# Attention beside chunk products: one place for TensorE's small work in a step, and lone 16-key tiles joined

## What is computed

```python
q, k, v, fg = hn @ w_q, hn @ w_k, hn @ w_v, hn @ w_f + b_forget
for q0, q1 in blocks:              # 16 meta rows, then four blocks of 128 queries
    s = q[q0:q1] @ k[:q1].T * 64 ** -0.5 + cum[q0:q1] - cum[:q1]   # forget gates' log sums
    p = softmax(where(causal, s, -inf))
    out[q0:q1] = p @ v[:q1]        # block [q0, q1) reads keys [0, q1)
```

## Time and profile before

| | us |
|---|---|
| median of 3 runs (911.46 to 912.39) | 911.9 |
| the profiled execution | 911.48 |
| its span, first to last instruction | 909.5 |
| TensorE busy | 900.1 |
| VectorE busy | 614.1 |
| ScalarE busy | 445.0 |
| GpSimd busy | 22.3 |

### The profile page before, as it was taken

One profiled execution on the slowest core, in us unless ns is written; L12 is line 12 of the kernel. 1 busy time (PEld: TensorE's weight loads), 2 busy tenths in 40 slices (PEclk: granted clock), 3 DMA queues, 4 the chain that ended last, 5 costly groups with the idle time before them and its releaser, 6 DMA issues.

```text
span 909.5 us, 13686 instructions
## 1 busy us (share of the span) xinstructions
PE 900.1 (99%) x5039; PEld 784.2 (86%) x5039; DVE 614.1 (68%) x959; ACT 445.0 (49%) x722; POOL 22.3 (2%) x40
## 2 busy tenths in 40 slices
PE   8999999999999999999999999999999999999997
PEld 7999999899999999888888888888888888888886
DVE  7799989999999999987765444533443354334543
ACT  6532246777778777766843244421243133214523
POOL 2010000000000000010000000000000000000000
PEclk9999999999999999999999999999999999999999
DMA  9333332212221222213323532323233333333602
GB/s 267 93 98 92 92 93 70 70 49 70 70 68 48 70 70 54 81 52 92 116 82 104 186 92 85 101 94 100 87 100 108 92 92 92 115 93 98 179 1 93
DMA packets 129466, 84.34 MB, mean 93 GB/s; under 512 B 3103, under 2 KB 118815, under 8 KB 129424
## 3 DMA queue, kind: packets, MB, share of 16 engines
q1 hardware_dynamic: 128192, 82.32, 31.1%
q10 hardware_dynamic: 640, 1.18, 0.4%
q0 software_dynamic: 592, 0.29, 0.2%
HBM read 81.62 MB, written 2.16 MB: 92 GB/s over the span
## 4 chain that ended last, share of the span: by engine, by line
PE 92%; DVE 4%; ACT 2%; issue 1%; DMA 1%; SPq 0%; ACTq 0%
PE pj L1455 41%; PE pQ L1707 19%; PE pj L1451 17%; PE pQ L1585 3%; PE pQ L1602 3%; PE pj L1773 2%; PE pQ L1773 2%; PE pj L1493 1%; DVE cv L1051 1%; PE pQ L1572 1%; PE pQ L1571 1%; DVE w_lo L955 1%; DMA ga<-in_x_dram 1%; ACT w_hi L577 1%; PE pQ L1605 1%
## 5 line engine op out<-in xcount | busy, mean ns | idle before, releaser
L955 DVE TENSOR_TENSOR w_lo<-raw,w_hi 128x1024 fp32r<-128x1024 f32 x129 | 157.6, 1222 | 113.5 <-ACT w_hi L577 113.2
L577 ACT ACTIVATE w_hi<-raw 128x1024 fp32r<-128x1024 f32 x129 | 135.9, 1053 | 161.5 <-PE pQ L1707 121.3
L1455 PE MATMUL pj<-in_hi,w_lo 128*128 128x512 f32 x512 | 201.5, 394 | 0.0
L1455 PE MATMUL pj<-in_lo,w_hi 128*128 128x512 f32 x512 | 200.6, 392 | 0.0
L1455 PE MATMUL pj<-in_hi,w_hi 128*128 128x512 f32 x512 | 200.1, 391 | 0.2 <-DVE w_lo L955 0.2
L1051 DVE SCALAR_TENSOR_TENSOR cv<-u,prm,cv 128x512 f32<-128x512 f32 x240 | 170.6, 745 | 0.5
L1455 PEld LDWEIGHTS pj<-in_hi,w_hi 128*128 128x128 f32 x512 | 96.3, 188 | 19.5 <-DVE w_lo L955 0.6
L1455 PEld LDWEIGHTS pj<-in_lo,w_hi 128*128 128x128 f32 x512 | 96.2, 188 | 17.8
L1455 PEld LDWEIGHTS pj<-in_hi,w_lo 128*128 128x128 f32 x512 | 96.3, 188 | 17.2
L1707 PE MATMUL pQ<-w_hi,mid_hi 128*128 128x512 f32 x256 | 99.8, 390 | 0.0
L1707 PE MATMUL pQ<-w_lo,mid_hi 128*128 128x512 f32 x256 | 99.6, 389 | 0.0
(11 more groups left out here) (206 smaller groups left out, 1226.1 us busy)
## 6 DMA issues: line engine op xcount, KB each, us to landing
raw<-in_w_in_dram SPq DMA_DIRECT2D x57, 512.0 KB, 3.8
raw<-in_w_mlp_up_dram SPq DMA_DIRECT2D x32, 512.0 KB, 4.0
raw<-in_w_mlp_down_dram SPq DMA_DIRECT2D x32, 512.0 KB, 3.8
raw<-in_w_attn_out_dram SPq DMA_DIRECT2D x8, 512.0 KB, 3.6
raw<-in_w_conv_out_dram SPq DMA_DIRECT2D x8, 512.0 KB, 3.6
raw<-in_w_out_dram SPq DMA_DIRECT2D x8, 512.0 KB, 3.9
ga<-in_x_dram SPq DMA_DIRECT2D x4, 512.0 KB, 8.4
cv<-in_x_dram SPq DMA_DIRECT2D x1, 2048.0 KB, 9.1
```

Source lines behind the costliest of these rows:

```text
L577: A(w_hi[:, c % SPLIT, :], raw[:, c % RAW, :], ACT.Copy).then_inc(s_hi, 1)
L955: V.tensor_tensor(w_lo[:, c % SPLIT, :], raw[:, c % RAW, :], w_hi[:, c % SPLIT, :].bitcast(F32), ALU.subtract).then_inc(s_lo, 1)
L1455: last = mm(prod(c), wt, src[:, at:at + NT], **flags)
```

## The change

TensorE: CUTS becomes (0, 4, 12), and everything small stands after unit 4 of a step, in the order transposes, half_out, value transposes, scores. The transposes are now those of the unit two steps back instead of one, and half_out moves from steps 3, 5, 7 and 1 to 4, 6, 0 and 2. The lone tiles: the fifth key tile's 16 probabilities are put by ScalarE into `lone_probs`, behind 32 columns of zeros, and turned from there (48 columns instead of 128); the fifth value tile holds the keys of two lone tiles, 16 rows each at rows 0 and 32. So in the second half_out of a head one product of 256 columns for each part serves block 1's lone tile and block 3's together, and line 1605's products go.

ScalarE and VectorE: other orders in the steps, other numbers of taps, `normalise` of 528 keys and the copy of V in two instructions each. Not shown: four one-column tensors become columns of one, and the same reordering in ScalarE's step of k = 8.

```diff
-TAPS_FIRST_PAIR = (2, 3, 2, 2, 2, 2, 3, 2)
-TAPS_STEP = {18: (3, 4, 1, 2, 1, 2, 3, 2), 19: (3, 4, 1, 2, 2, 2, 3, 2)}
+TAPS_FIRST_PAIR = (3, 4, 2, 2, 1, 3, 1, 2)
+TAPS_STEP = {18: (1, 3, 3, 3, 1, 3, 2, 2), 19: (1, 3, 3, 4, 1, 3, 2, 2)}
...
-FIRST_CELL = (0, 2, 0, 4)
-CELLS = 9
+FIRST_CELL = (0, 2, 0, 5)
+CELLS = 10
+LONE_ROW = 32
...
+        with ExitStack() as row_gap:
+            lone_probs = row_gap.enter_context(nc.sbuf_tensor("lone_probs", [P, LONE_ROW + META], F32))
...
+        def probs_cell(q, t):
+            return lone_probs[:, :] if (q, t) == (QT - 1, QT) else probs(q, t * P, (t + 1) * P)
...
+        def lone_values(c):
+
+            at = AT + 2 * P
+            return pj[:, c % 2, at:at + 4 * P].rearrange("p (a b) -> p a b", b=2 * P)[:, :, 0:META]
...
@@ -671,7 +681,11 @@
                 U = 8 * k + s
                 wait(act, s_rinv, U + 1, it, 16)
                 nk = META + P * (s % QT + 1)
-                A(probs(s % QT, 0, nk), probs(s % QT, 0, nk), ACT.Copy, scale=rinv[:, s:s + 1]).then_inc(s_pn, 1)
+                last = A(probs(s % QT, 0, min(nk, NT)), probs(s % QT, 0, min(nk, NT)), ACT.Copy, scale=rinv[:, s:s + 1])
+                if nk > NT:
+                    last = A(lone_probs[:, LONE_ROW:], probs(s % QT, NT, nk), ACT.Copy,
+                             scale=rinv[:, s:s + 1])
+                last.then_inc(s_pn, 1)
...
-                    A(vT[:, 0:T], prod(c - 1, T), ACT.Copy).then_inc(s_vev, 1)
+                    A(vT[:, 0:NT], prod(c - 1, T)[:, 0:NT], ACT.Copy)
+                    A(vT[:, NT:VT].rearrange("p (a b) -> p a b", b=LONE_ROW)[:, 0:2, 0:META],
+                      lone_values(c - 1), ACT.Copy).then_inc(s_vev, 1)
...
-                if s == 3 and k >= 2:
-                    out_high(k - 2, it)
-                turned_out(s, k, it)
-                if s == 2 and k >= 2:
-                    out_copy(1, k - 2, it)
                 if s == 6:
                     projection_out(s, k, it)
                 if s % 2 == 0 and c > N_PAIR:
                     high(c + 1, it, 8)
+                if s == 2:
+                    if k >= 2:
+                        out_copy(1, k - 2, it)
+                    if live:
+                        values_high(k - 1, it)
+                if s != 6:
+                    turned_out(s, k, it)
+                if s == 3:
+                    projection_out(s, k, it)
+                    if k >= 2:
+                        out_high(k - 2, it)
+                if live:
+                    exponential(s, k - 1, it)
                 if s == 4:
                     projection_out(s, k, it)
-                if s == 3 and k == 1:
-                    projection_out(s, k, it)
+                    second_copy(s, k, it)
+                if s == 6:
+                    turned_out(s, k, it)
                 if live:
-                    exponential(s, k - 1, it)
+                    normalise(s, k - 1, it)
                 if s == 0:
                     projection_out(s, k, it)
-                if s == 2 and live:
-                    values_high(k - 1, it)
-                if s == 3 and k != 1:
-                    projection_out(s, k, it)
-                if s == 6 and live:
-                    out_copy(0, k - 1, it)
-                if s in (4, 6):
+                if s == 6:
                     second_copy(s, k, it)
-                if live:
-                    normalise(s, k - 1, it)
+                    if live:
+                        out_copy(0, k - 1, it)
...
             for k in (PAIRS + 1,):
                 for s in range(8):
                     c = N_PAIR + 4 * k + s // 2
-                    turned_out(s, k)
-                    if s == 2:
-                        out_copy(1, k - 2)
-                    if s == 3:
-                        out_high(k - 2)
                     if s % 2 == 0:
                         gate_out(s, k)
                         high(c + 1)
                     if s == 0:
                         act.wait_ge(s_csum, KT + 1)
                         A(sum_parts[0], conv_sum[:, :], ACT.Copy).then_inc(s_sumhi, 1)
+                    turned_out(s, k)
+                    if s == 2:
+                        out_copy(1, k - 2)
+                    if s == 3:
+                        out_high(k - 2)
...
+            V.memset(lone_probs[:, 0:LONE_ROW], 0.0).then_inc(s_one, 1)
...
                 if s == 0:
+                    row_least(s, k - 1)
+                    taps(s, k, 0, 1)
+                    turned_low(s, k)
+                    sum_reciprocal(s, k - 1)
+                    low(c + 1)
+                    taps(s, k, 1, None)
+                elif s == 1:
                     taps(s, k, 0, 1)
                     row_least(s, k - 1)
+                    taps(s, k, 1, 2)
                     turned_low(s, k)
-                    taps(s, k, 1, 2)
-                    sum_reciprocal(s, k - 1)
-                    taps(s, k, 2, 3)
-                    low(c + 1)
-                elif s == 1:
-                    turned_low(s, k)
-                    row_least(s, k - 1)
-                    taps(s, k, 0, 2)
                     sum_reciprocal(s, k - 1)
                     taps(s, k, 2, None)
                 elif s == 2:
+                    taps(s, k, 0, 2)
+                    low(c + 1)
+                    row_least(s, k - 1)
+                    values_low(k - 1)
                     turned_low(s, k)
+                    sum_reciprocal(s, k - 1)
+                    taps(s, k, 2, None)
+                elif s == 3:
                     if k >= 2:
                         out_add(1, k - 2)
+                    taps(s, k, 0, 1)
                     row_least(s, k - 1)
-                    low(c + 1)
+                    taps(s, k, 1, 2)
+                    turned_low(s, k)
                     sum_reciprocal(s, k - 1)
-                    taps(s, k, 0, None)
-                    values_low(k - 1)
-                elif s == 3:
-                    if k == 1:
-                        turned_low(s, k)
-                    row_least(s, k - 1)
-                    if k > 1:
-                        turned_low(s, k)
-                    taps(s, k, 0, 1)
-                    sum_reciprocal(s, k - 1)
-                    taps(s, k, 1, 2)
+                    taps(s, k, 2, None)
                     if k >= 2:
                         out_low(k - 2)
                 elif s == 4:
+                    row_least(s, k - 1)
                     taps(s, k, 0, 1)
                     turned_low(s, k)
+                    sum_reciprocal(s, k - 1)
+                    low(c + 1)
+                    if k < PAIRS:
+                        projection_low(s, k)
+                    taps(s, k, 1, None)
+                elif s == 5:
                     row_least(s, k - 1)
-                    low(c + 1)
+                    taps(s, k, 0, 1)
+                    turned_low(s, k)
                     sum_reciprocal(s, k - 1)
                     taps(s, k, 1, None)
-                    if k < PAIRS:
-                        projection_low(s, k)
-                elif s == 5:
+                elif s == 6:
+                    taps(s, k, 0, 1)
                     row_least(s, k - 1)
-                    turned_low(s, k)
-                    taps(s, k, 0, None)
-                    sum_reciprocal(s, k - 1)
-                elif s == 6:
-                    taps(s, k, 0, 3)
-                    row_least(s, k - 1)
-                    turned_low(s, k)
                     if k < PAIRS:
                         projection_low(s, k)
                     sum_reciprocal(s, k - 1)
-                    out_add(0, k - 1)
+                    turned_low(s, k)
+                    taps(s, k, 1, None)
                     low(c + 1)
                 else:
+                    row_least(s, k - 1)
                     turned_low(s, k)
-                    row_least(s, k - 1)
-                    taps(s, k, 0, 1)
+                    out_add(0, k - 1)
                     sum_reciprocal(s, k - 1)
-                    taps(s, k, 1, 2)
+                    taps(s, k, 0, None)
...
             k = PAIRS + 1
             for s in range(8):
-                turned_low(s, k)
                 if s % 2 == 0:
                     low(N_PAIR + 4 * k + s // 2 + 1)
                 if s == 0:
                     dve.wait_ge(s_sumhi, 1)
                     V.tensor_tensor(sum_parts[1], conv_sum[:, :], sum_parts[0].bitcast(F32), ALU.subtract).then_inc(s_sumlo, 1)
+                turned_low(s, k)
                 if s == 6:
                     dve.wait_ge(s_sqhi, 1)
                     V.tensor_tensor(sq_parts[1], sq_sum, sq_parts[0].bitcast(F32), ALU.subtract).then_inc(s_sqlo, 1)
                 if s == 1:
                     dve.wait_ge(s_mus, 1)
-                if s == 2:
-                    out_add(1, k - 2)
                 for m in CENTRED_AT.get(s, ()):
```

(76 more changed lines are left out.)

## The result

The changed kernel takes 915.59 us (median, 914.18 to 916.76), the kernel before 911.78 beside it. The ratio is 1.0038, 95% interval 1.0029 to 1.0048. Forecast were 911.2 and a range of 907.0 to 914.2. The profiled execution took 915.78 us, 4.30 more than that of before.

What follows compares the result with a forecast made beforehand. The prediction took TensorE as the bound, busy 900.1 of 909.5 us, with VectorE next. Savings of 5.6 us and new waits of 4.9 gave -0.7, so 911.9 became 911.2 us, range 907.0 to 914.2.

Steps and rivals of the forecast that it cites:

- Lone products: TensorE, each head: four lone products of 128 columns become two of 256, 3.2 us less over 16 heads.
- Lone transpose: TensorE, each head: the lone transpose by rows gets cheaper, 0.4 us less in all, bounds 0 and 0.8.
- Joining: TensorE leaves the chunk stream 8 times a pair instead of 17, 0.7 us less, bounds 0 and 1.4.
- Old waits recovered: Old-order waits that go: 0.97 us extra in the first pair, 0.35 in pairs with 19 taps; together 1.3.
- first pair: First pair of heads: VectorE's tap backlog delays turned_low, so TensorE waits 2.7 us; the old 0.97 extra goes.
- New waits: TensorE waits the new order adds: first pair 2.7, step 5 0.9, last steps 1.3; together 4.9 us.
- step 5: Step 5: a tap waiting for GpSimd's add delays turned_low; 0.13 us in five pairs, 0.23 in pair 8, 0.9 total.
- spread: TensorE's spread of the conv-channel mean, after the last pair, waits for late last taps and GpSimd adds; 1.3 us.
- rival (c): Last steps: first issued of tap and GpSimd add wins, so the last tap holds the add; 911.7 us, chance 0.11.
- (a): Rival: the new waits don't come in this size, only step 5's 0.9 stays; 907.2 us, chance 0.30.
- (b): Rival: ScalarE 0.5 us late in step 6 makes seven pairs lose 0.42 each; 914.1 us, chance 0.18.
- (d): Rival: one place instead of three saves TensorE nothing, 0.4 and 0.7 fall away; 912.3 us, chance 0.10.

Runs made afterwards that it cites:

- e9: Changed kernel with first-pair taps respread, step 5's turned_low ahead of its tap, pair 8's step 7 taps and the orders behind pair 8 rearranged; 908.37 us.
- e10: e9 without the joined lone tiles: block 3's lone tile again has its own 128-column transposes and products, one copy each for normalise and V; 911.15 us.
- e1: Changed kernel with the first pair's taps spread otherwise, fewer ahead of the wait, same total work; 911.89 us.
- e4: Changed kernel with ten unused products of 512 columns ahead of the transposes that wait in the first pair's step 3; 914.20 us.
- e2: Changed kernel with pair 8's two taps of step 7 done in step 4 instead; 914.93 us.
- e8: e1 with pair 8's first step 7 tap behind row_least and, after pair 8, units ahead of sums, out_add ahead of centred values; 909.45 us.
- e6: e1 with turned_low of step 5 ahead of the first tap instead of behind it; 910.84 us.
- e5: Kernel before, its places and orders kept, with only the lone tiles joined; 910.13 us.

## Why the prediction was wrong

**Lone products, 3.2: right.** e9's pair is 0.38 us shorter than e10's (32.77 to 32.39), 8 pairs, 3.0 us; the times differ by 2.8. This difference holds the lone transposes too, and the next rows give them nothing of it.

**Lone transpose, 0.4: nothing.** Here is the changed kernel at the place shown for e10, TensorE and its weight loads:

```profile
222.79 0.60 PE L1607 MATMUL pQ<-ident,prob 128*128 128x128 f32 x4
223.11 0.10 PEld L1607 LDWEIGHTS pQ<-ident,lone_probs 128*48 128x48 f32 x1
223.22 0.19 PEld L1593 LDWEIGHTS pQ<-k_a,q_a 128*128 128x128 f32 x1
...
223.59 0.40 PE L1473 MATMUL pj<-in_lo,w_hi 128*128 128x264 f32 x2
```

From the first transpose to the next chunk product it is 0.80 us (222.79 to 223.59), and 0.80 with five full ones (219.55 to 220.35). The record of the 48-column weight load is shorter, 0.10 for 0.19, but the next load starts 0.11 behind it all the same. The Trainium skill (TensorE: Matmul & The Clock Gate, "LDWEIGHTS") has the load's cost follow its columns; as a cadence this run doesn't show it.

**Joining, 0.7: nothing**, by e10. The excess of 0.02 us for a departure was read from rows with two decimals.

**Old waits recovered, 1.3: the 19-tap part (0.35) right; of the first pair's 0.97, less than half.** In e9 and e1, where the new wait of 2.7 is evened out, the first pair is still 0.54 above a steady one, so 0.43 is recovered. In the changed kernel the new wait stands in the place of the whole 0.97, and the table counts it so.

**New waits: the first pair and step 5 right, the spread too small, and the list too short.** This is the step that failed: "New waits: 2.7 + 0.9 + 1.3 = 4.9 us." By the traces of before and after:

| term | forecast | measured | from |
|---|---|---|---|
| lone products | -3.2 | -3.0 | 8 x 0.38 |
| lone transpose, joining | -1.1 | 0 | e10 |
| 19-tap pairs | -0.35 | -0.35 | e10 |
| first pair, wait | 2.7 - 0.97 | 2.9 - 0.97 | 145.67 to 148.80, less 0.23 |
| first pair, clock behind it | none | 1.5 | 36.78 - 32.39 - 2.9; e4 has 1.4 |
| step 5 | 0.9 | 0.8 | five pairs 0.10 to 0.15, pair 8 0.2 |
| spread | 1.3 | 2.25 | timeline; 0.35 of it stays in e2 |
| w_lo in the gate chunks | none | 1.5 | timeline, e8 |
| sum | -0.7 | 4.6 | 4.30 in the profiles; 0.3 stays unexplained |

Three things were missed. The clock: the prediction priced TensorE's standing still at its length alone. The wait for w_lo: the part on the last steps followed the chain to the spread and stopped there, and neither `out_add` behind the centred values in step (2, 9) nor the mean's copy behind `turned_out` in step (1, 9) was followed into what queues behind it. And the adds: rival (c) had the rule, and it applied to both adds, where it was priced for one; the Trainium skill (SBUF — State Buffer, "Who interferes with whom") states it, and the 1.75 us against 1.30 agree. The gains were 1.1 us too high besides.

Of the rivals, (a) is refuted by the waits; (b) by the pairs without a wait in step 7; (c) and (d) were right as mechanisms and wrong as to where the time ends, since each let only one term fall. That the change itself could be a gain is shown by e9; that it takes the taps' numbers and three orders to get it, by e1 and e6 to e8.

## What to carry to other kernels

When work is moved in orders written by hand, follow every moved instruction into the queue behind it on its own engine up to the end of the stage, not only along the chain that is known to be critical; here a moved `out_add` and a mean's copy that came late cost 1.5 us through three engines. Price a stall of TensorE with what the clock may take after it, and test it by filling the stall with unused products. Before the places of small products are merged, measure what a departure costs: here it was nothing, and all the gain lay in four products a head becoming two.

## Hardware behaviour that was not expected

- The granted clock fell to half for 3.4 us behind a wait of 2.7 us (in both profiles that have it at full length, after and e2) and behind one of 1.85 in one profile (e1) of four that have such a wait (after, e1, e4 and e6); e8 and e9, with 1.2, kept it full. The length of the wait doesn't decide it alone: in the opening stage the clock fell in e5's profile behind a wait of 1.13 and stayed full in e6's behind one of 1.63. The cost is about 1.4 us, 7 products of 512 columns 0.43 apart instead of 0.23. Of seven runs of the changed kernel the fastest, 914.18 us, is the one whose mean clock was 1.000; the slowest, 916.76, has 0.995. What decides behind the shorter waits is left open.
- A GpSimd add of two SBUF tensors takes 1.73 to 1.75 us instead of 1.29 when a tap or a `low` was issued 0.1 to 0.6 us ahead of it (after, e1, e4, e6), and 1.56 in e2, where a tap had been running for 0.33. A tap issued into an add takes 1.02 and 1.52 (after) or 1.61 (before) instead of 0.75.
- A weight load of 48 columns instead of 128 has a record half as long and saves nothing from start to start (0.11 us).
